# Two-block model forward pass, feed-forward gate and up blocks: the low half of two of eight chunks made by a negated rounding and an accumulating transfer

## The chip, the core and the metric

The kernel runs on one core of one Trainium2 chip. The metric is the device time of one execution in microseconds, the median of three runs. All arithmetic is in 32-bit floating point; the matrix products run on TensorE in its float32r form, which keeps fewer bits of each factor.

## The reference, cut to what matters

The program computes two layers of a hybrid attention model (`first_block`) and then one layer of another (`second_block`) for 256 tokens of width 2048. The change touches only the last part, the feed-forward network of the second block, with D_FF = 5632:

```python
gt, up = jnp.split(rms_norm_2(x, g_ffn) @ w_gate_up, 2, axis=-1)
return x + (jax.nn.silu(gt) * up) @ w_down
```

Everything before it (projections, attentions, gates) is many products of the same kind, activations times a streamed weight matrix.

## The kernel before, in words

**Tiles.** A block is 512 output columns of one weight matrix for all 256 tokens. Its weights are streamed in chunks. A plain chunk of 512 KB holds two row groups of 128 rows by 512 columns, 1024 numbers on each of 128 partitions. The gate and up blocks (names `gt` and `up`, 11 each) have 8 chunks, s = 0 to 7; the down blocks (4 for each j) have 2.

**Two halves.** To be as exact as the reference, each number w is split into a high half, w rounded to float32r, and a low half, w minus the high half. A product is three matmuls: activations' high half by the weights' high half, high by low, and low by high. A chunk is thus 2 row groups x 2 token groups x 3 = 12 matmuls of 128x128 by 128x512.

**One chunk's way.** SP (`load`, L698 on) brings the raw weights into one of four raw slots. ScalarE (`split`, L1108 on, instruction at L1121) writes the high half into `w_hi`. VectorE (`split`, L1408 on, instruction at L1418) subtracts it from the raw weights and writes the low half into `w_lo`. TensorE (L1100) multiplies. All four engines count: `raw_landed` per slot, `hi_done`, `lo_done` and `mm_done` over all chunks. Raw, `w_hi` and `w_lo` each have four slots in this stage, so that chunk c+4 uses the slots of chunk c. ScalarE waits for `mm_done` of chunk c-4 before it writes the halves of chunk c; TensorE waits for `lo_done` of chunk c; SP waits, before it loads into a raw slot, for `lo_done` of the chunk that was in it. SP issues the loads strictly in order, and stands at the first one whose wait is not met.

**Order of the feed-forward blocks.** gate 0, up 0; then for j = 0 to 8 gate j+1, the four down blocks of j, up j+1; then gate 10, up 10, down 9, down 10. In all 22 x 8 + 44 x 2 = 264 chunks. Other work is put between chunks by a schedule written out by hand (`schedule`): after an up block, `h_feed` turns (transposes) its product on TensorE (L808, four matmuls) after the next block's s = 2 and s = 3, and ScalarE and VectorE copy it. Each engine does read-outs of finished blocks after it has split the chunk four further on.

**The start of the stage.** The scale of the norm before the feed-forward network comes from the squares of x. ScalarE takes them in four parts (`x_sq`, L1267) as the last output blocks end, the last part at the second chunk of gate 0. GpSimd then computes the scale in `x_norm(3)`, four small instructions, the last thing that its program does. It is needed only when gate 0 is read out. Turns of x (`x_feed`) come after s = 1 and s = 2 of gate 0. GpSimd issues no transfer anywhere in the kernel.

Of the kernel before, what the change touches and what calls it, by code (L numbers as in the profile page):

```python
# [201 lines left out]
SPLIT_OF = {r: c for c, (_b, _w, _s, r) in enumerate(UNITS) if r is not None}  # L202
R_BEHIND = [max(U_PREV[:c + 1]) for c in range(N_CHUNKS)] + [N_CHUNKS]
BEHIND = {c: range(max(R_BEHIND[c], 0), R_BEHIND[c + 1]) for c in range(N_CHUNKS)}
EXT_FIRST = {l: [min(c for c in range(FIRST_WIDE[l], N_CHUNKS) if U_SLOT[c] == k) for k in (4, 5)] for l in range(DEPTH)}
EXT_LOAD = {l: min(r for r, (b, _s) in enumerate(LOADS) if b >= FIRST_PANEL[l] and R_SLOT[r] >= RING) for l in range(DEPTH)}
BLOCK = {b.name: i for i, b in enumerate(BLOCKS)}
# [3 lines left out]
def end_of(*name):  # L211
    return BLOCKS[BLOCK[name]].end
# [197 lines left out]
def hybrid_program(nc, x, mem_by_col, w_in, w_mem_kv, w_branch, w_out, w_in2, b_gate, w_uq, w_ukv, w_o_mla, w_o_dil, w_o2, w_gu, w_down,  # L410
                   pars_d, x_by_col, k_ident, k_levels, k_tables, k_dil, x_kept, mkv_kept, out):
    with ExitStack() as ctx:
# [162 lines left out]
        sums_done, forms_ready, forms_done, form_rounded = sem("sums_done"), sem("forms_ready"), sem("forms_done"), sem("form_rounded")  # L575
        crossed, x_banks_free, wide_sig = sem("crossed"), sem("x_banks_free"), sem("wide_sig")
        hi_done, lo_done, mm_done = sem("hi_done"), sem("lo_done"), sem("mm_done")
        gm_free = [sem(f"gm_free{i}") for i in range(2)]
        pt_full, pt_hi = sem("pt_full"), sem("pt_hi")
        pt_free = [sem(f"pt_free{i}") for i in range(2)]  # L580
# [114 lines left out]
        def _(sp):  # L695
            def load(r):
                b, s = LOADS[r]
                blk = BLOCKS[b]  # L698
                if R_PREV[r] >= 0:
                    sp.wait_ge(lo_done, SPLIT_OF[R_PREV[r]] + 1)  # L700
                    if LOADS[R_PREV[r]] in LOAD_SUMS:
                        sp.wait_ge(sums_done, 2 * LOAD_SUMS[LOADS[R_PREV[r]]] + 2)
                if r in EXT_LOAD.values():
                    sp.wait_ge(y_ready, Y_OF["s_pv", "m", blk.name[1], H - 1] + 1)
                k = R_SLOT[r]
                to = slot_of(raw, raw_more, k)[:, 0:blk.ck * blk.width].rearrange("p (j n) -> p j n", n=blk.width)
                sp.dma_start(to, cut(weights[blk.weights], blk.ck)[s, :, :, blk.col:blk.col + blk.width]).then_inc(raw_landed[k], 16)
# [15 lines left out]
                sp.dma_start(rows(x_kept)[:, :, n * NB:(n + 1) * NB], xs[:, :, n * NB:(n + 1) * NB]).then_inc(x_saved, 16)  # L723

            def back(l):
                sp.wait_ge(lo_done, SUMS_UNIT[LAST_PANEL[l], SEVEN[-1]] + 1)
                if l:
                    sp.wait_ge(x_saved, 64 * l)
                sp.dma_start(xs, rows(x[0] if l == 0 else x_kept)).then_inc(x_back, 16)
# [6 lines left out]

            def bring_mkv():
                sp.wait_ge(mkv_out, 16)
                sp.wait_ge(lo_done, end_of("merge", 0, "b", 3))
                sp.dma_start(arena[:, 11408:13456].rearrange("p (i n) -> p i n", n=NB),  # L740
                             mkv_kept.rearrange("i (t p) n -> p (i t) n", p=P)).then_inc(mkv_in, 16)

# [57 lines left out]
        def _(pe):  # L800
# [235 lines left out]
            def panel(b, blk):  # L1036
                l, n = blk.name[1], PANEL_N[b]
                if n:
                    pe.wait_ge(x_banks_free, 2 * n)
                if b == FIRST_PANEL[l]:  # L1040
                    turned(pe, PT_OF["tail", "b", l, H - 1])
                    pe.wait_ge(ps_free, PS_OF["b_qk", l, H - 1] + 1)
                    pe.wait_ge(y_ready, Y_OF["norm", "b", l, H - 1] + 1)
                    pe.wait_ge(forms_done, len(SEVEN) * (l + 1))
                for c in range(blk.first, blk.end):
                    _b, what, s, _r = UNITS[c]
                    first, last = s == SEVEN[0], s == SEVEN[-1]
                    pe.wait_ge(lo_done, c + 1)
                    if what == "low":
                        three(PT[0], *by_token(2 * s + 1, 0), c, 0, False, False)  # L1050
                        mm = three(PT[1], *by_form(s, 3), c, 1, False, False)
                    elif what == "first":
                        if first:
                            pe.wait_ge(gm_free[0], blk.before[0])
                        mm = three(G[0][:, 0, :], *by_token(2 * s, 0), c, 0, first, last)
                    elif what == "sums13":
                        three(G[0][:, 1, :], *by_form(s, 0), c, 0, first, last)
                        if first:
                            pe.wait_ge(gm_free[1], blk.before[1])
                        mm = three(G[1][:, 0, :], *by_form(s, 2), c, 1, first, last)  # L1060
                    elif what == "sums24":
                        three(G[1][:, 1, :], *by_form(s, 1), c, 0, first, last)
                        mm = three(PS, *by_token(2 * s + 1, 1), c, 1, False, False)
                    else:
                        end = s == KD - 1
                        for t, banks in enumerate(((PT[0], PT[1]), (PS, PO))):
                            for h, bank in enumerate(banks):
                                mm = three(bank, *by_token(s, t), c, h, c == blk.first, end)
                    mm.then_inc(mm_done, 1)
                    between(c)  # L1070

            for b, blk in enumerate(BLOCKS):
                if blk.kind == "panel":
                    panel(b, blk)
                    continue
                ah, al = (xh, xl) if blk.pair == "x" else (yh, yl)
                if blk.before[blk.g]:
                    pe.wait_ge(gm_free[blk.g], blk.before[blk.g])
                for s in range(blk.chunks):
                    c = blk.first + s  # L1080
                    fed = need(blk.name, s)
                    if fed:
                        turned(pe, PT_OF[fed])
                    if blk.name == ("mk", 0):
                        pe.wait_ge(mem_fed, s + 1)
                    if blk.name == ("a_qi", 0):
                        pe.wait_ge(first_fed, s + 1)
                        pe.wait_ge(ident_in, 16)
                    pe.wait_ge(lo_done, c + 1)
                    for j in range(blk.ck):  # L1090
                        k = s * blk.ck + j
                        if blk.kind == "turned":
                            for q, (a, w) in enumerate(((ah, high_of), (ah, low_of), (al, high_of))):
                                mm = M.matmul(G[blk.g][0:blk.width, 0, 0:T], ringed(w, blk, c)[:, j, :], a[:, blk.kk + k, :],  # L1094
                                              start=(k == 0 and q == 0), stop=(k == blk.kt - 1 and q == 2))
                            continue
                        for t in range(TT):
                            tok = slice(t * P, (t + 1) * P)
                            for q, (a, w) in enumerate(((ah, high_of), (ah, low_of), (al, high_of))):
                                mm = M.matmul(G[blk.g][:, t, :], a[:, blk.kk + k, tok], ringed(w, blk, c)[:, j, :],  # L1100
                                              start=(k == 0 and q == 0), stop=(k == blk.kt - 1 and q == 2))
                    mm.then_inc(mm_done, 1)
                    between(c)

        @block.scalar
        def _(act):
            A = nc.scalar.activation

            def split(c):
                b, what, s, r = UNITS[c]  # L1110
                if r is None:
                    act.wait_ge(sums_done, 2 * SUMS_N[b, s] + (1 if what == "sums13" else 2))
                else:
                    act.wait_ge(raw_landed[R_SLOT[r]], 16 * (R_COUNT[r] + 1))
                if U_PREV[c] >= 0:
                    act.wait_ge(mm_done, U_PREV[c] + 1)
                for l in range(DEPTH):
                    if c in EXT_FIRST[l]:
                        act.wait_ge(y_ready, Y_OF["norm", "b", l, H - 1] + 1)
                        act.wait_ge(o_squared, NORM_OF["norm", "b", l, H - 1] + 1)  # L1120
                A(high_of(c)[:, 0:size_of(c)], source_of(c), ACT.Copy).then_inc(hi_done, 1)  # L1121

            def stem(b):
                _, l, br, m = BLOCKS[b].name
# [259 lines left out]
        def _(dve):  # L1384
# [9 lines left out]
            def sums13(n, r):  # L1394
                for k in (r, r + 1):
                    dve.wait_ge(raw_landed[R_SLOT[k]], 16 * (R_COUNT[k] + 1))
                if n >= 2:
                    dve.wait_ge(lo_done, SUMS_UNIT[SUMS[n - 2]] + 1)
                q = pair_of(r)
                V.tensor_tensor(sums[:, n % 2, 0:2, :], q[:, :, 1, :], q[:, 0, :, :], ALU.subtract).then_inc(sums_done, 1)  # L1400

# [5 lines left out]

            def split(c):  # L1408
                b, what, s, r = UNITS[c]
                if what == "low":  # L1410
                    sums13(SUMS_N[b, s], r - 1)
                elif what == "first":
# [329 lines left out]
        def _(pool):  # L1742
# [149 lines left out]
            for i in range(2):  # L1892
# [2 lines left out]
                    freed(pool, BLOCK[f"ukv{2 * i + j}", 2])  # L1895
                head_norm(f"k{i}", 2, k_h[:, :, 4 * i:4 * i + 4, 0:P], 4)
            x_norm(3)


def packed(inputs):  # L1900
# [33 lines left out]
```

## Time and profile before

| | |
|---|---|
| median of 3 runs | 3288.4 us (3288.28 to 3288.69) |
| span of the profiled execution | 3286.7 us |
| TensorE busy | 3274.1 us, 100% |
| VectorE busy | 2052.8 us, 62% |
| ScalarE busy | 1577.0 us, 48% |
| GpSimd busy | 307.5 us, 9% |
| HBM traffic | 188 GB/s over the span |

The span is from the first to the last instruction in the profile; it lies 1.7 us under the median of the runs. TensorE's matmuls are pipelined, so the busy time of one (0.39 us) overlaps the next; the time from start to start is the pace. "L1100" is line 1100 of the kernel.

### The profile page before, as it was taken

Reading aid. Unit: us, or ns where it says so; the run is one execution under the profiler, and the core shown is the slowest. Engines: PE = TensorE matmul, PEld = TensorE weight load, DVE = VectorE, ACT = ScalarE, POOL = GpSimd, SP = SyncE. Lnnn points to the kernel's source line nnn. Section 1 sums busy time; section 2 is a strip of 40 time slices with the busy share of each in tenths; the row PEclk is TensorE's granted clock in tenths of the full one; section 3 lists DMA queues with packets and bytes.
Section 4 is the critical chain, followed back from the end, with each engine's and each line's share of the span. In section 5 each row is a group of like instructions: output and inputs, shape, how many; then the busy total and the mean of one; then the engine's idle time right before and its main releaser. Section 6 shows DMA issues by size and latency. Waiting matters only on the chain.

```text
span 3286.7 us, 39565 instructions
## 1 busy us (share of the span) xinstructions
PE 3274.1 (100%) x15172; PEld 2714.8 (83%) x15172; DVE 2052.8 (62%) x2284; ACT 1577.0 (48%) x1992; POOL 307.5 (9%) x267
## 2 busy tenths in 40 slices
PE   9999999999999999999999999999999999999999
PEld 7888888888888888888888888888888888888887
DVE  5466655588865656555888655575555555555555
ACT  6454445455544444454555445455444444444443
POOL 0111241100001102411000010160000000000000
PEclk9999999999999999999999999999999999999999
DMA  8665555665656655556666675554665666666665
GB/s 300 193 185 165 166 175 162 192 209 189 228 182 200 184 167 167 172 165 190 201 202 201 202 219 168 167 180 151 194 191 184 187 191 192 192 187 191 192 192 167
DMA packets 303805, 619.76 MB, mean 189 GB/s; under 512 B 24960, under 2 KB 29440, under 8 KB 302464
## 3 DMA queue, kind: packets, MB, share of 16 engines
q1 hardware_dynamic: 303616, 617.22, 61.4%
q8 instruction: 121, 1.98, 0.2%
q14 instruction: 68, 0.56, 0.1%
HBM read 609.80 MB, written 7.34 MB: 188 GB/s over the span
## 4 chain that ended last, share of the span: by engine, by line
PE 100%; DMA 0%; DVE 0%; ACT 0%; SPq 0%; issue 0%
PE G L1100 80%; PE X L1025 3%; PE X L1027 3%; PE X L1026 3%; PE X L808 2%; PE G L1027 1%; PE G L1026 1%; PE G L1025 1%; PE X L921 1%; PE X L893 1%; PE G L1094 1%; PE X L948 0%; PE X L947 0%; PE X L914 0%; PE X L895 0%; PE X L868 0%
## 5 line engine op out<-in xcount | busy, mean ns | idle before, releaser
L1418 DVE TENSOR_TENSOR w_lo<-raw,w_hi 128x1024 fp32r<-128x1024 f32 (+1 forms) x1016 | 1255.4, 1237 | 1149.1 <-ACT w_hi L1121 1125.9
L1121 ACT ACTIVATE w_hi<-raw 128x1024 fp32r<-128x1024 f32 (+1 forms) x1016 | 1067.1, 1052 | 1448.8 <-PE G L1100 1376.5
L1100 PE MATMUL G<-w_hi,xh 128*128 128x512 f32 x2560 | 1021.8, 399 | 0.0
L1100 PE MATMUL G<-w_hi,xl 128*128 128x512 f32 x2560 | 999.4, 390 | 0.0
L1100 PE MATMUL G<-w_lo,xh 128*128 128x512 f32 x2560 | 996.9, 389 | 0.0
L1100 PEld LDWEIGHTS G<-w_hi,xl 128*128 128x128 f32 x2560 | 480.5, 188 | 103.6
L1100 PEld LDWEIGHTS G<-w_hi,xh 128*128 128x128 f32 x2560 | 481.1, 188 | 95.6 <-issue 2.7
L1100 PEld LDWEIGHTS G<-w_lo,xh 128*128 128x128 f32 x2560 | 481.6, 188 | 94.3
L1100 PE MATMUL G<-w_hi,yh 128*128 128x512 f32 x1256 | 497.3, 396 | 8.2 <-DVE w_lo L1418 8.2
L1100 PE MATMUL G<-w_hi,yl 128*128 128x512 f32 x1256 | 490.7, 391 | 0.0
L1100 PE MATMUL G<-w_lo,yh 128*128 128x512 f32 x1256 | 489.7, 390 | 0.0
L1100 PEld LDWEIGHTS G<-w_hi,yh 128*128 128x128 f32 x1256 | 236.5, 188 | 55.0 <-issue 8.2
L1100 PEld LDWEIGHTS G<-w_hi,yl 128*128 128x128 f32 x1256 | 236.2, 188 | 50.5
L1100 PEld LDWEIGHTS G<-w_lo,yh 128*128 128x128 f32 x1256 | 236.6, 188 | 47.5
L1025 PE MATMUL X<-w_hi,xh 128*128 128x512 f32 x340 | 132.8, 390 | 0.0
L1027 PE MATMUL X<-w_hi,xl 128*128 128x512 f32 x340 | 132.7, 390 | 0.0
L1026 PE MATMUL X<-w_lo,xh 128*128 128x512 f32 x340 | 132.4, 389 | 0.0
L1759 POOL TENSOR_TENSOR stat<-stat 128x4 f32<-128x4 f32 x4 | 0.8, 203 | 1250.6 <-ACT core L1267 1250.6
L1418 DVE TENSOR_TENSOR w_lo<-raw_more,w_hi 128x1024 fp32r<-128x1024 f32 (+1 forms) x56 | 64.9, 1165 | 27.6 <-ACT w_hi L1121 27.6
L1121 ACT ACTIVATE w_hi<-raw_more 128x1024 fp32r<-128x1024 f32 (+1 forms) x56 | 56.2, 1014 | 48.6 <-PE X L1027 38.3
L808 PE MATMUL X<-ident,arena 128*128 128x128 f32 x512 | 77.1, 272 | 0.0
L808 PEld LDWEIGHTS X<-ident,arena 128*128 128x128 f32 x512 | 63.3, 140 | 15.2
(248 smaller groups left out, 2782.2 us busy)
## 6 DMA issues: line engine op xcount, KB each, us to landing
raw<-in_w_in SPq DMA_DIRECT2D x572, 512.0 KB, 3.6
raw<-in_w_gate_up SPq DMA_DIRECT2D x176, 512.0 KB, 3.6
raw<-in_w_down SPq DMA_DIRECT2D x88, 512.0 KB, 3.6
raw<-in_w_out SPq DMA_DIRECT2D x64, 512.0 KB, 3.9
raw_more<-in_w_in SPq DMA_DIRECT2D x52, 512.0 KB, 4.3
raw<-in_w_branch SPq DMA_DIRECT2D x48, 512.0 KB, 3.9
raw<-in_w_mem_kv SPq DMA_DIRECT2D x32, 512.0 KB, 6.0
raw<-in_w_o SPq DMA_DIRECT2D x32, 512.0 KB, 3.7
```

The source lines that it names most:

```text
L808: mm = M.transpose(PT[i % 2][0:n, col:col + P], src, ident[:])
L893: mm = M.matmul(PS[:, t * T:(t + 1) * T], qk_t[:, t * P:(t + 1) * P], qk_t[:, T:2 * T], start=True, stop=br != "l")
L921: mm = M.matmul(PO[:, t * P:(t + 1) * P], p_t[:, a, t * P:(t + 1) * P], v(a), start=(a == 0), stop=(a == TT - 1))
L1025: M.matmul(bank, of_h, high_of(c)[:, cols], start=start, stop=False)
L1026: M.matmul(bank, of_h, low_of(c)[:, cols], start=False, stop=False)
L1027: return M.matmul(bank, of_l, high_of(c)[:, cols], start=False, stop=stop)
L1094: mm = M.matmul(G[blk.g][0:blk.width, 0, 0:T], ringed(w, blk, c)[:, j, :], a[:, blk.kk + k, :], start=(k == 0 and q == 0), stop=(k == blk. ...
L1100: mm = M.matmul(G[blk.g][:, t, :], a[:, blk.kk + k, tok], ringed(w, blk, c)[:, j, :], start=(k == 0 and q == 0), stop=(k == blk.kt - 1 and ...
L1121: A(high_of(c)[:, 0:size_of(c)], source_of(c), ACT.Copy).then_inc(hi_done, 1)
L1418: V.tensor_tensor(low_of(c)[:, 0:n], source_of(c), high_of(c)[:, 0:n].bitcast(F32), ALU.subtract).then_inc(lo_done, 1)
L1759: link(V.tensor_tensor(s[:, 0:4], s[:, 0:4], s[:, 4:8], ALU.add))
```

## The change

In each gate and up block, chunks s = 2 and s = 6 (`ADDED`, 44 in all) get their low half another way. VectorE skips them. ScalarE, right after the high half, writes the rounded weights once more with scale -1 into `w_lo` and counts `lo_negative`. GpSimd, after everything else in its program, waits for that count and issues a transfer from the raw slot to `w_lo` that adds what it brings to what is there, so that w_lo becomes raw minus high half. Its landing adds 16 to `lo_added`. TensorE waits for `lo_added` at these chunks, and SP waits for it before it loads into their raw slots. As VectorE now counts 44 chunks fewer, every other wait on `lo_done` goes by `lows(n)`, n less the added chunks before n.

```diff
+ADDED = [c for c, (b, _w, s, _r) in enumerate(UNITS) if BLOCKS[b].name[0] in ("gt", "up") and s % 4 == 2]
+ADDED_N = {c: i for i, c in enumerate(ADDED)}
+def lows(n):
+    return n - sum(1 for c in ADDED if c < n)
...
                 if R_PREV[r] >= 0:
-                    sp.wait_ge(lo_done, SPLIT_OF[R_PREV[r]] + 1)
+                    if SPLIT_OF[R_PREV[r]] in ADDED_N:
+                        sp.wait_ge(lo_added, 16 * (ADDED_N[SPLIT_OF[R_PREV[r]]] + 1))
+                    else:
+                        sp.wait_ge(lo_done, lows(SPLIT_OF[R_PREV[r]] + 1))
...
-                    pe.wait_ge(lo_done, c + 1)
+                    if c in ADDED_N:
+                        pe.wait_ge(lo_added, 16 * (ADDED_N[c] + 1))
+                    else:
+                        pe.wait_ge(lo_done, lows(c + 1))
...
                 A(high_of(c)[:, 0:size_of(c)], source_of(c), ACT.Copy).then_inc(hi_done, 1)
+                if c in ADDED_N:
+                    A(low_of(c)[:, 0:size_of(c)], source_of(c), ACT.Copy, scale=-1.0).then_inc(lo_negative, 1)
...
             def split(c):
                 b, what, s, r = UNITS[c]
+                if c in ADDED_N:
+                    return
...
             x_norm(3)
+            for i, c in enumerate(ADDED):
+                pool.wait_ge(lo_negative, i + 1)
+                V.dma_start(low_of(c).bitcast(F32), source_of(c), accum_op=ALU.add).then_inc(lo_added, 16)
```

## Rows read from the trace of the kernel before

**Rows 1.** The page, part 1: busy us, share of the span, instructions.
```profile
PE 3274.1 (100%) x15172; PEld 2714.8 (83%) x15172; DVE 2052.8 (62%) x2284; ACT 1577.0 (48%) x1992; POOL 307.5 (9%) x267
```

**Rows 2.** The page, part 4: the chain that ended last, by engine.
```profile
PE 100%; DMA 0%; DVE 0%; ACT 0%; SPq 0%; issue 0%
```

**Rows 3.** Waits, whole span: who waited for whom, us, times, longest.
```profile
PE G L1100 <- DVE w_lo L1418: 8.2, 1, 8.2
```

**Rows 4.** Waits between 2562 and 3260 us, all that is listed.
```profile
ACT w_hi L1121 <- PE G L1100: 405.3, 253, 2.0
DVE w_lo L1418 <- ACT w_hi L1121: 300.5, 253, 1.8
```

**Rows 5.** The chain in order of time: start, us, what, matmuls.
```profile
2675.22 62.59 PE G L1100 x276
```

**Rows 6.** Timeline: start, us, engine, line, one subtraction and matmuls around it.
```profile
2587.49 1.23 DVE L1418 TENSOR_TENSOR w_lo<-raw,w_hi 128x1024 fp32r<-128x1024 f32 x1 [1.50 <-ACT w_hi L1121]
2587.50 0.39 PE L1100 MATMUL G<-w_hi,xh 128*128 128x512 f32 x1
...
2587.73 0.39 PE L1100 MATMUL G<-w_lo,xh 128*128 128x512 f32 x1
...
2588.86 0.39 PE L1100 MATMUL G<-w_hi,xh 128*128 128x512 f32 x1
...
2589.09 0.39 PE L1100 MATMUL G<-w_lo,xh 128*128 128x512 f32 x1
```

**Rows 7.** Timeline of ScalarE; in brackets its idle time and releaser.
```profile
2602.72 1.06 ACT L1121 ACTIVATE w_hi<-raw 128x1024 fp32r<-128x1024 f32 x1 [1.66 <-PE G L1100]
2605.44 1.06 ACT L1121 ACTIVATE w_hi<-raw 128x1024 fp32r<-128x1024 f32 x1 [1.66 <-PE G L1100]
2606.41 0.58 ACT L1216 ACTIVATE yh<-X 128x512 fp32r<-128x512 f32 x1
```

**Rows 8.** Transfers, whole span: queue, count, KB each, median us to landing.
```profile
arena<-x_kept SPq DMA_DIRECT2D x2, 2048.0 KB, 9.2
...
out<-arena SPq DMA_DIRECT2D x4, 512.0 KB, 2.7
...
tables<-const_dil SPq DMA_DIRECT2D x1, 512.0 KB, 7.3
```

**Rows 9.** The weight loads (line 707) between 2675 and 2741 us.
```profile
L707 SPq DMA_DIRECT2D raw<-in_w_gate_up x16: 367/367/368, 2691.3 to 2732.1; - x16
...
DMA to landing us min/median/max: 3.5/3.7/4.1
```

**Rows 10.** Timeline of GpSimd: first and last instruction of x_norm(3).
```profile
2560.66 0.20 POOL L1759 TENSOR_TENSOR stat<-stat 128x4 f32<-128x4 f32 x1 [345.36 <-ACT core L1267]
...
2561.55 0.70 POOL L1754 TENSOR_TENSOR stat<-stat 128x2 f32<-128x2 f32 x1
```

**Rows 11.** One period of 24 chunks: busy us, clock, DMA share, GB/s.
```profile
2675.00:2741.24 66.24, 66.24 (x300) 54.86 (x297) 37.81 (x34) 27.59 (x29) 0.00 (x0) 1.00 0.64 191
```

**Rows 12.** Timeline of ScalarE at the start of gate 0.
```profile
2558.24 1.06 ACT L1121 ACTIVATE w_hi<-raw 128x1024 fp32r<-128x1024 f32 x1 [1.67 <-PE G L1100]
...
2560.34 0.19 ACT L1267 ACTIVATION_READ_ACCUMULATOR core<-arena 128x1 f32 x1
```

**Rows 13.** The chain around gate 0's s = 2.
```profile
2551.78 6.36 PE G L1100 x28
2558.14 0.44 PE X L808 x4
2558.58 2.76 PE G L1100 x12
```

**Rows 14.** Timeline of TensorE's matmuls at the kernel's start.
```profile
8.19 0.77 PE L1100 MATMUL G<-w_hi,yh 128*128 128x512 f32 x1 [8.19 <-DVE w_lo L1418]
8.75 0.63 PE L1100 MATMUL G<-w_lo,yh 128*128 128x512 f32 x1
9.18 0.63 PE L1100 MATMUL G<-w_hi,yl 128*128 128x512 f32 x1
...
12.16 0.41 PE L1100 MATMUL G<-w_hi,yh 128*128 128x512 f32 x1
12.42 0.39 PE L1100 MATMUL G<-w_lo,yh 128*128 128x512 f32 x1
```

More of the change, by code:

```diff
@@ L577, in hybrid_program @@
         hi_done, lo_done, mm_done = sem("hi_done"), sem("lo_done"), sem("mm_done")
+        lo_negative, lo_added = sem("lo_negative"), sem("lo_added")
         gm_free = [sem(f"gm_free{i}") for i in range(2)]
@@ L725, in back @@
             def back(l):
-                sp.wait_ge(lo_done, SUMS_UNIT[LAST_PANEL[l], SEVEN[-1]] + 1)
+                sp.wait_ge(lo_done, lows(SUMS_UNIT[LAST_PANEL[l], SEVEN[-1]] + 1))
                 if l:
@@ L738, in bring_mkv @@
                 sp.wait_ge(mkv_out, 16)
-                sp.wait_ge(lo_done, end_of("merge", 0, "b", 3))
+                sp.wait_ge(lo_done, lows(end_of("merge", 0, "b", 3)))
                 sp.dma_start(arena[:, 11408:13456].rearrange("p (i n) -> p i n", n=NB),
@@ L1088, in _ @@
                         pe.wait_ge(ident_in, 16)
-                    pe.wait_ge(lo_done, c + 1)
+                    if c in ADDED_N:
+                        pe.wait_ge(lo_added, 16 * (ADDED_N[c] + 1))
+                    else:
+                        pe.wait_ge(lo_done, lows(c + 1))
                     for j in range(blk.ck):
@@ L1397, in sums13 @@
                 if n >= 2:
-                    dve.wait_ge(lo_done, SUMS_UNIT[SUMS[n - 2]] + 1)
+                    dve.wait_ge(lo_done, lows(SUMS_UNIT[SUMS[n - 2]] + 1))
                 q = pair_of(r)
```

## The prediction

> **What bounds the kernel now.** I read the busy shares, the chain that ended last, the waits, and then the timelines of the feed-forward stage, engine by engine. TensorE is busy for 3274.1 of 3286.7 us and the chain runs through it alone [rows 1, 2]. Its one wait for VectorE's low half is the 8.2 us before the first chunk of the whole kernel [rows 3]. From 2562 to 3260 us, nearly all of the changed stage, no wait of TensorE is listed: what is listed there is ScalarE waiting for TensorE to free a w_hi slot, 253 times [rows 4]. So VectorE's subtraction is not late anywhere that this change touches it. The stage runs at TensorE's own pace: 276 matmuls in 62.59 us, 0.2268 us each [rows 5], so a chunk (12 matmuls) takes 2.72 us and four take 10.88. The pitch is the same beside a VectorE subtraction (2587.50 to 2587.73) and after it (2588.86 to 2589.09) [rows 6].
>
> **How much lead a low half has.** With four slots, chunk c's rounding starts 0.1 us after chunk c-4's last matmul, three chunks (8.16 us) before TensorE wants chunk c. Today high half 1.06 plus low half 1.23 us leave well over 5 us of cover.
>
> **What the change removes.** 44 VectorE subtractions (22 blocks x 2) of 1.23 us, 54 us of an engine that waits for ScalarE anyway. On the path they are worth 0, hidden behind TensorE's 100%. I bound the gain by the pitch below (second rival).
>
> **What it adds on ScalarE.** 44 negated roundings of 1.06 us. Back to back, ScalarE's next instruction starts 0.97 us after the first [rows 7], so the negated half is ready 0.97 + 1.06 + 0.07 for the semaphore = 2.1 us after the rounding starts. ScalarE idles 1.66 us between roundings, so 1.06 more fits. Behind it are queued the read-outs and transposed copies of h; those are wanted chunks later, cost 0.
>
> **What it adds on GpSimd and the DMA.** 44 accumulating transfers of 512 KB. Call D the time from GpSimd being free to issue until the sum has landed. The trace has no accumulating transfer and no transfer issued by GpSimd, so D is bounded by rows. Below: the fastest 512 KB landing, the output's 2.7 us [rows 8]. Above: the 2 MB copy, 9.2 us for four times the bytes; another 512 KB table took 7.3 [rows 8]. For the value: the weight loads of this stage land in 3.7 us [rows 9]. Between 512 KB and 2 MB that is (9.2 - 3.7) / 3 = 1.83 us per 512 KB over a fixed 1.9. An addition must read both operands, twice the bytes: 1.9 + 2 x 1.83 = 5.5. GpSimd's small instructions take 0.2 us [rows 10]; I add that for issuing and take D = 5.7 as an estimate. The engines are there: DMA share is 0.64 in this stage [rows 11], and while an accumulation runs SP stands behind it (below), so it runs nearly alone.
>
> The doubling agrees with the Trainium skill, Collectives: The Full Stack, Stop 4, which says a reduction costs "two source reads" and puts the slowdown there, not in the adder. Against it stands DMA: Bandwidth & Descriptors, the SWDGE anatomy, with about 2.0 us plus bytes over 436 GB/s, and no charge for adding: 3.2 us. No row here can show either; by that formula everything below the first chunk would be hidden, which is the first rival.
>
> **The first added chunk is certain to stall.** GpSimd's program issues the transfers after x_norm(3), which needs ScalarE's last squares, which end at 2560.5 [rows 12], and itself ends at 2561.55 + 0.70 = 2562.25 [rows 10]. The first added chunk is s = 2 of the first gate block, and TensorE starts it at 2558.58 (its s = 1 ends at 2558.14, a turn of 0.44 follows) [rows 13]. Nothing upstream of x_norm(3) needs that chunk, so it isn't a deadlock, but TensorE stands still from 2558.58 to 2562.25 + D: 3.67 + 5.7 = 9.4 us. After the 8.19 us of standing still at the kernel's start the matmuls came 0.43 us apart, 512 columns at the 1.2 GHz level, until 12.16 and 0.23 apart after it [rows 14]; the nine from 8.19 to 12.16 took 3.97 us instead of 2.04. I charge the same 1.9 here. Sum: 11.3 us. Nothing later gives it back, since TensorE has no idle time to give.
>
> **The other 43.** Two tests, in the lead's terms. The slot path: 0.1 + 2.1 + D against 8.16, so an undisturbed chunk is late by D - 5.9. The raw path: the next load into this raw slot (chunk c+4) now waits in SP for lo_added, and c+4 is again an added chunk (s = 2, 6, 2, 6), also from one block into the next. From one sum landed to the next: 0.1 + 3.7 load + 0.1 + 2.1 + D = D + 6.0 against 10.88, so each further link adds D - 4.9 to the lateness (before, that load went out 2.4 us after the slot came free and landed at 6.2, 4.7 us ahead of its use). SP's loads for the three plain chunks queue behind that wait, but their halves have 5 us of cover, cost 0. In a gate block after an up block two turns (0.88 us) lie between s = 2 and s = 6, so that link adds D - 5.8. A down block's eight plain chunks end the run. The order of blocks gives gate 0, up 0, gate 1 (six links), eight times up, gate (four), then up 9, gate 10, up 10 (six).
> At D = 5.7 a run of four: -0.2, then 0.6, 1.4, 1.3: TensorE loses 1.4, eight times, 11.2. The first run, after its stall: its second link has one turn, 0.4, then 1.2, 2.0, 2.8, 2.7: 2.8. The last: -0.2, 0.6, 1.4, 1.3, 2.1, 2.9: 2.9. Together 16.9 us.
>
> **Sum.** 11.3 + 16.9 = 28.2 us on a span of 3286.7; the profiled span lies 1.7 us under the runs' median of 3288.4, and I carry that over: 3316.6. The sum is steep in D. At 4.9 and under only the first stall is left; at 7.3 the terms are 12.9 + 8 x 7.7 + 10.7 + 12.5 = 98, so 3386; at 9.2 they are 14.8 + 8 x 15.3 + 20.2 + 23.9 = 181, so 3470.
>
> **Rivals.**
> First, the transfer is covered: D at most 4.9. Then the loss is 3.67 + D + 1.9, at D = 4 some 9.6: 3298 (3297 to 3299). For it: the output's 2.7 us. Against: it has to read twice and no load here lands under 3.5 [rows 9].
> Second, on the other side, not slower: TensorE's pitch of 0.227 us is over the 0.213 that 0.427 at the lower clock level [rows 14] halves to. If VectorE's port traffic made that difference, quiet chunks would gain 12 x 0.0135 = 0.16 us each, 7 us over 44 chunks, 43 over all 264 of the stage. It decides once more than 70 chunks speed up, since the first stall costs 11.3; with all 264 it gives 3288.4 + 11.3 - 43 = 3257 where the transfers are covered. Against: the pitch does not move when VectorE stops within a chunk [rows 6], and VectorE is relieved in 44 chunks only.
> Third, the adding is slow: D above 6.5, so nearly all links are late, 3350 to 3470; 3386 at the 7.3 row. For it: an adder's rate and the software side of GpSimd's queue show in no row. TensorE idling a few us over and over could bring the lower clock level back each time, which adds to it.
>
> **Chances.** The forecast (D 4.9 to 6.5, 3299 to 3350) 0.45; covered, 0.25; slow adding, 0.26; not slower, 0.04. The measurement tells 0.2%, 6.6 us, from no change: faster 0.01, same 0.03, slower 0.96. The range: from 3296 (D near 3 and a milder clock) to 3410 (D near 7.7), leaving about 0.04 below and 0.15 above.
>
> **What would show it.** A TensorE gap before gate 0's s = 2 that ends D after x_norm(3), and matmuls 0.43 us apart behind it. Waits of TensorE for the transfer, longest at the end of a run of added chunks, none in down blocks. ScalarE's rounding of the later links waiting for the raw load, not for TensorE. 44 fewer VectorE subtractions with an unchanged pitch of 0.227. Wrong would be: no gap there (the first term), a GpSimd transfer that lands outside 4.9 to 6.5 us (the second), or a pitch that moved.

## The result, and the profile after

The changed kernel takes 3302.8 us (median of four, 3300.1 to 3303.4) against 3288.55: 14.3 us more, a ratio of 1.0041 (95% interval 1.0030 to 1.0053). The direction and the stall at the first added chunk came as forecast, the losses at the other 43 mostly did not; the whole is half of the 28.2 us that the sum gave. The profiled execution has a span of 3300.6 us.

The page of the changed kernel, against [rows 1, 2]: part 1 (busy us, share, instructions), GpSimd's queue from part 3 (packets, MB, share of the 16 engines), the chain by engine from part 4, and from part 6 the transfers (KB each, median us to landing).

```profile
PE 3278.6 (99%) x15172; PEld 2718.6 (82%) x15172; DVE 1999.7 (61%) x2240; ACT 1617.5 (49%) x2036; POOL 345.7 (10%) x311
...
q0 software_dynamic: 6336, 23.07, 3.7%
...
PE 97%; DMA 2%; ACT 1%; issue 0%; DVE 0%; POOL 0%; SPq 0%; ACTq 0%; POOLq 0%
...
raw<-in_w_gate_up SPq DMA_DIRECT2D x176, 512.0 KB, 4.4
...
w_lo<-raw POOLq DMA_DIRECT2D x44, 512.0 KB, 4.5
```

VectorE has 44 instructions and 53 us less, ScalarE 44 more, and a second queue carries 23 MB. What is new for the time is the 2% of the chain that hangs on a transfer. It lies in few places. The waits between 2562 and 3275 us, where [rows 4] had none of TensorE's (PEld is TensorE's weight load, which meets the wait first; the two rows are the same stalls):

```profile
ACT w_hi L1137 <- PE G L1116: 312.8, 215, 11.6
ACT w_hi L1137 <- DMA raw<-in_w_gate_up: 51.7, 22, 3.3
...
PEld G L1116 <- DMA w_lo<-raw: 11.4, 6, 8.6
PE G L1116 <- DMA w_lo<-raw: 8.9, 2, 8.4
```

**The first added chunk.** The chain in order of time (start, us, what) runs where the prediction drew it: ScalarE's last squares, GpSimd's four instructions of x_norm(3), the transfer, and only then s = 2 of gate 0:

```profile
2559.81 1.33 ACT core L1285 x4
...
2562.15 0.65 POOL stat L1774
2562.80 4.72 DMA w_lo<-raw
2567.52 0.04 issue
2567.56 5.49 PE G L1116 x12
2573.05 0.55 PE X L821 x4
```

Before, TensorE started this chunk 0.44 us after s = 1 and spent 2.76 us on it [rows 13]. Here s = 1 ends at 2558.58 and the turn, 0.44 us as before, at 2559.02, so it stands still 8.5 us, and the 12 matmuls then take 5.49. The windows of TensorE's granted clock say why (us, busy of PE, PEld, DVE, ACT, POOL, then clock, DMA share, GB/s):

```profile
2567.56:2573.36 5.80, 5.80 (x17) 4.54 (x17) 0.00 (x0) 0.00 (x0) 0.00 (x0) 0.52 0.84 283
2573.60:2617.19 43.59, 43.59 (x195) 36.03 (x194) 18.24 (x18) 22.46 (x24) 3.45 (x4) 1.00 0.74 216
```

0.52 is the 1.2 GHz level. Chunk and turn take 5.80 us where they took 3.20, so the clock costs 2.6 and the place 8.5 + 2.6 = 11.1 us.

**The other 43.** From 2620.8 to 2661.7, and again over most of the stage, TensorE runs without a stall. One period of 24 chunks, against [rows 11]:

```profile
2875.00:2941.24 66.24, 66.24 (x297) 54.88 (x296) 32.99 (x30) 31.37 (x33) 3.78 (x5) 1.00 0.76 225
```

VectorE is busy 5 us less, the DMA share is up from 0.64 to 0.76, TensorE is full as before. And 276 matmuls of one stretch take 62.60 us (62.59 in [rows 5]): the pitch has not moved. Five short waits of the weight load follow the first one; four of them show between matmuls, 0.2 to 0.7 us each, 1.5 in all, with some 0.1 us of a slower first matmul behind each. Matched one by one with the matmuls of the kernel before, those of this execution lose 2.0 us between the first added chunk and the end. The prediction expected the longest waits at the end of a run of added chunks; of these four only the one at 2692.6 is there. The chain into it:

```profile
2664.19 5.07 DMA w_lo<-raw
2669.25 0.02 issue
2669.27 3.89 DMA raw<-in_w_gate_up
2673.16 0.02 issue
2673.19 1.06 ACT w_hi L1137
2674.25 0.96 ACT w_lo L1139
2675.20 0.28 issue
2675.49 4.51 DMA w_lo<-raw
2680.00 0.02 issue
2680.02 4.00 DMA raw<-in_w_gate_up
...
2686.43 6.16 DMA w_lo<-raw
2692.59 0.04 issue
```

This is the raw path, link by link: sum landed, load 3.9 to 4.0, two roundings 2.0, release of GpSimd 0.3 to 0.4, sum 4.5. From 2669.25 to 2680.00 is 10.75 us against the 10.88 that TensorE takes for four chunks. A link of ordinary length thus adds nothing. The long sums make the stall: had the last one taken 4.5 us and not 6.16, or the first 4.5 and not 5.07, the 0.3 us for which TensorE stands still at 2692.6 would be covered.

### The profile page after: what moved, and what is told of

It reads as the page before. It is cut to its first block, busy times and chain, and to the rows that moved or that the text cites. A ratio compares the mean times of both kernels' runs of the same rounds, so it can differ in the third digit from the quotient of the medians.

```text
span 3300.6 us, 39565 instructions
## 1 busy us (share of the span) xinstructions
PE 3278.6 (99%) x15172; PEld 2718.6 (82%) x15172; DVE 1999.7 (61%) x2240; ACT 1617.5 (49%) x2036; POOL 345.7 (10%) x311
## 4 chain that ended last, share of the span: by engine, by line
PE 97%; DMA 2%; ACT 1%; issue 0%; DVE 0%; POOL 0%; SPq 0%; ACTq 0%; POOLq 0%
PE G L1116 78%; PE X L1038 3%; PE X L1040 3%; PE X L1039 3%; PE X L821 2%; DMA w_lo<-raw 1%; PE G L1040 1%; PE G L1039 1%; PE G L1038 1%; DMA raw<-in_w_gate_up 1%; PE X L934 1%; PE X L906 1%; PE G L1110 1%; PE X L961 0%; PE X L960 0%; PE X L927 0%
## 5 line engine op out<-in xcount | busy, mean ns | idle before, releaser
L1438 DVE TENSOR_TENSOR w_lo<-raw,w_hi 128x1024 fp32r<-128x1024 f32 (+1 forms) x972 | 1201.3, 1238 | 1165.5 <-ACT w_hi L1137 1142.2
L1920 POOL DMA_DIRECT2D w_lo<-raw x44 | 38.4, 872 | 640.2 <-ACT w_lo L1139 640.2
```

What stands on the lines that cost most here:

```text
L1438: V.tensor_tensor(low_of(c)[:, 0:n], source_of(c), high_of(c)[:, 0:n].bitcast(F32), ALU.subtract).then_inc(lo_done, 1)
L1920: V.dma_start(low_of(c).bitcast(F32), source_of(c), accum_op=ALU.add).then_inc(lo_added, 16)
```

## The experiments

Each is the changed kernel with the edit shown. Times are medians. The kernel before was timed beside each: 3288.55 for the first four, 3288.65 for "The same, unchained" and for the chunk at s = 4, and 3288.87 for the other four.

**GpSimd's order.**
```diff
-            x_norm(3)
             for i, c in enumerate(ADDED):
+                if i == 1:
+                    x_norm(3)
                 pool.wait_ge(lo_negative, i + 1)
```


> All 44 added chunks stay; GpSimd issues the first transfer before x_norm(3) instead of after it. Theory A (of the 14.3 us lost, 11.2 are the first chunk: 8.5 us standing behind x_norm(3) and 2.6 us at the lower clock level; the rest is the links of the raw slot): that gap is gone and the total is 3291.5 (3290 to 3293). Rival B (the loss is spread over the 44 transfers: issue, contention, pitch): the gap's place changes little, 3300 or more.

Measured: 3292.0 us, ratio 1.0009 (1.0000 to 1.0019). The transfer goes out at 2552.44, x_norm(3) follows, the long gap is gone. Moving one line of GpSimd's program gives back 10.8 of the 14.3 us.

**The first chunk alone.**
```diff
-... s % 4 == 2]
+... s % 4 == 2][:1]
```


> Only the first of the 44 chunks (s = 2 of gate 0) is made by the transfer, the other 43 by VectorE as before. A: 3288.5 + 11.2 = 3299.7, TensorE idle 8.5 us once and 12 matmuls 0.43 us apart. B (loss spread over 44): 3289.

Measured: 3299.5 us, 1.0033 (1.0020 to 1.0046): 11.0 us from one transfer. That this equals the 11.1 us of the changed kernel is in part chance. In this profile TensorE stands still for the same 8.5 us, but only six matmuls run slowly, from 2567.85 to 2570.58, and not the whole chunk and the turn:

```profile
2570.15 0.63 PE L1116 MATMUL G<-w_hi,xl 128*128 128x512 f32 x1
2570.58 0.46 PE L1116 MATMUL G<-w_hi,xh 128*128 128x512 f32 x1
2570.87 0.39 PE L1116 MATMUL G<-w_lo,xh 128*128 128x512 f32 x1
```

So the lower clock costs 1.3 us here and 2.6 there. Another 0.9 us of this execution's loss was there before the changed stage began (see the last part of the account below).

**All but the first.**
```diff
-... s % 4 == 2]
+... s % 4 == 2][1:]
```


> The first of the 44 chunks goes back to VectorE, the other 43 keep the transfer. A: only the later links are left, 3288.5 + 1.9 to 3.0 = 3291, no fall of the clock. B: 3302.

Measured: 3290.5 us, 1.0006 (0.9997 to 1.0015). Forty-three transfers cost 1.9 us (1.4 by the matmuls of the profile), and 11.0 + 1.9 is 12.9 of 14.3. The spread loss (B) falls three times over.

**No two in a row.**
```diff
-... s % 4 == 2]
+... s == 2][1:]
```


> Added chunks only at s = 2 of each gate and up block, and not in gate 0: 21 transfers, never two in a row on one raw slot. A, with chaining through the raw slot as the cause of the later stalls: none is left, 3288.5 (within 0.5). Rival C (the later stalls come from the slot path alone, each transfer now and then landing late): half of them stay, 3289.5 to 3290.

Measured: 3290.0 us, 1.0003 (0.9994 to 1.0013), where I had expected 3288.5 from chaining and 3289.5 to 3290 from single late landings. By the time this one leans to rival C, but 1 us is at the edge of what these runs tell: in the profiled execution (3290.8 us) 1.4 us of the difference lie ahead of the changed stage and 0.8 in it. The profile is the firmer evidence. It has one stall on a transfer, and no chain can lead to it, so A's "none is left" does not hold:

```profile
PEld G L1116 <- DMA w_lo<-raw: 0.9, 1, 0.9
```

**The lead cut by one rounding.** This puts the other 43 back to about the D that the prediction assumed.
```diff
                 if c in ADDED_N:
+                    A(low_of(c)..., source_of(c), ACT.Copy, scale=-1.0).then_inc(neg_once, 1)
+                    act.wait_ge(neg_once, ADDED_N[c] + 1)
                     A(low_of(c)..., source_of(c), ACT.Copy, scale=-1.0).then_inc(lo_negative, 1)
```


> ScalarE writes the negated rounding of each added chunk twice, one after the other with a semaphore between, so each transfer starts some 1.15 us later; nothing else changes. This sets the lead back to about what the prediction assumed (its D of 5.7 against some 4.85 now, release included). A (chained links: load 3.9 to 5.1 + 2.1 + 0.35 + 4.5 + 1.15 against 10.88, each link adding 1.2 to 2.3 us): runs of four lose 3 to 4 us each and the runs of six 5 to 7, in all 3302.8 + 30 to 40, 3333 to 3343; by the prediction's own terms at D = 6.0, 3329. Rival C (only the slot path matters, 7.0 + 1.15 against 8.16): at most 0.1 per chunk, 3304 to 3307.

Measured: 3331.8 us, 1.0130 (1.0115 to 1.0145), 29.0 us over the changed kernel. A's 30 to 40 was a little high; C is far off. The prediction's own terms with D = 6.0 (4.5 + 0.35 + 1.1 as measured) give 0.1, 1.2, 2.3, 2.5 for a run of four, 4.2 and 4.7 for the long runs, 28.9 together; with the first stall of 11.1, which is not delayed by this, 3328.6. The later links measured 43.0 - 11.1 = 31.9 us over the kernel before, so the terms come out 3 us short. The waits of this kernel between 2560 and 3322 us:

```profile
ACT w_hi L1137 <- PE G L1116: 241.4, 166, 11.3
ACT w_hi L1137 <- DMA raw<-in_w_gate_up: 105.0, 32, 4.5
...
PEld G L1116 <- DMA w_lo<-raw: 44.2, 39, 8.6
```

39 waits instead of 6, and ScalarE waits twice as long for raw loads: those are the chained links.

**The same, unchained.** Both roundings, but only s = 2 and not in gate 0.

> The doubled negated rounding with 21 added chunks only (s = 2 of each block but gate 0), so that no two added chunks follow each other on one raw slot. A (the 29 us that the doubling cost with 44 chunks came through the chain sum, raw load, roundings, sum): an unchained chunk is at its limit, 8.2 against 8.16, loses 0 to 0.3: 3290.0 + 0 to 5, 3290 to 3295. Rival C (each delayed transfer costs by itself, 29 us over 43): 14 us, 3304.

Measured: 3295.2 us, 1.0019 (1.0009 to 1.0028), at the edge of what A allowed, and 8.8 us under C. Its waits between 2560 and 3280 us:

```profile
PEld G L1116 <- DMA w_lo<-raw: 7.9, 21, 0.6
```

All 21 are now late, by 0.38 us on average, the slot path at its limit. The prediction's terms give 0.1 us for such a chunk. The second rounding costs (3295.2 - 3290.0) / 21 = 0.25 us per chunk here and 29.0 / 43 = 0.67 in the chained kernel: the greater part of the loss there comes through the chain.

**What D is made of.** A copy in place of the addition:
```diff
-... source_of(c), accum_op=ALU.add).then_inc(lo_added, 16)
+... source_of(c)).then_inc(lo_added, 16)
```


> The 44 transfers copy the raw weights over w_lo instead of adding them: same bytes written, the addition and its second read left out (the low half is then wrong in value, the timing path the same). A (adding costs a second read, a 4 KB packet of 340 ns being two of 170): packets near 170 ns, issue to landing 3.1 instead of 4.5 us, the first gap 1.4 shorter, later stalls gone: 3299 to 3300. Rival D (340 ns is what a transfer from slot to slot issued by GpSimd costs): 4.5 us and 3302 to 3303 as before.

Measured: 3296.9 us, 1.0027 (1.0016 to 1.0038), below the forecast of 3299 to 3300. In the profile (3298.5 us) TensorE waits for a transfer once, at the first chunk, for 7.0 us; the later stalls are gone, as forecast. Nine matmuls run slowly there, fewer than in the changed kernel. Why the executions lie as far apart as 3296.4 and 3299.2 us no trace shows. Its line 1920, then the same for the changed kernel (duration ns min/median/max):

```profile
L1920 POOL DMA_DIRECT2D w_lo<-raw x44: 530/530/782, 2563.2 to 3236.6; - x44
...
DMA to landing us min/median/max: 2.8/2.9/5.2
```
```profile
L1920 POOL DMA_DIRECT2D w_lo<-raw x44: 852/862/1094, 2562.8 to 3240.5; - x44
...
DMA to landing us min/median/max: 4.5/4.5/6.2
```

A 4 KB packet takes a median of 160 ns copied and 340 ns added. A transfer has 128 of them, eight for each of the 16 engines if they are spread evenly: by that estimate the addition costs 8 x 0.18 = 1.4 us there, beside 0.33 us in issuing; between the landings lie 1.6 us.

**Half the bytes.**
```diff
-... low_of(c).bitcast(F32), source_of(c), accum_op ...
+... low_of(c)[:, 0:NB].bitcast(F32), source_of(c)[:, 0:NB], accum_op ...
```


> The 44 transfers add only the first 512 of the 1024 columns (the rest of the low half keeps the negated high half: its value is wrong). Splits the 4.5 us: A (1.43 to the first packet, 8 packets one after the other, 0.3 to the count, a packet's time going by its bytes): 2 KB packets of 170 ns, landing at 3.1 us. Rival D (time per packet fixed): 340 ns and 4.5 us.

Measured: landing at 3.3 us, 2 KB packets of 187 ns, issuing unchanged at 862 ns, 3298.5 us. Time goes mostly by bytes (A), with a small part per packet: 340 is less than 2 x 187. Here too TensorE waits for a transfer only once, at the first chunk.

**Where the clock falls.** One added chunk only, at s = 3, then at s = 4.
```diff
-... s % 4 == 2]
+... s == 3][:1]
```


> One added chunk only, s = 3 of gate 0 (not s = 2). TensorE reaches it at about 2562.2, the sum lands at 2567.5: idle 5.3 us. If the lower clock level follows that too: 3288.5 + 5.3 + 2.6 = 3296.4; if it does not: 3293.8.

> One added chunk only, s = 4 of gate 0. TensorE reaches it at about 2564.9, the sum lands at 2567.3: idle 2.4 us. After 8.5 and 5.3 us idle the matmuls came 0.427 us apart; if that follows an idle time this short too, 3288.6 + 2.4 + 2.6 = 3293.6, if not 3291.0 to 3291.5.

Measured: 3297.6 us (1.0026, 1.0015 to 1.0037) and 3291.7 us (1.0009, 1.0000 to 1.0019). The first matmul after the gap and the clock behind it, s = 3 and then s = 4:

```profile
2566.84 0.80 PE L1116 MATMUL G<-w_hi,xh 128*128 128x512 f32 x1 [5.22 <-DMA w_lo<-raw]
...
2566.84:2572.13 5.29, 5.29 (x12) 4.13 (x13) 0.00 (x0) 0.00 (x0) 0.00 (x0) 0.50 0.77 266
```
```profile
2567.58 0.50 PE L1116 MATMUL G<-w_hi,xh 128*128 128x512 f32 x1 [2.44 <-DMA w_lo<-raw]
...
2567.58:2572.00 4.42, 4.42 (x19) 3.67 (x20) 0.00 (x0) 0.87 (x1) 0.00 (x0) 1.00 0.76 254
```

After 5.2 us of standing still the next matmuls ran at 1.2 GHz; after 2.4 us they did not, here.

No version beat the kernel before. The best one that keeps transfers, at s = 2 alone, comes within 1.4 us of it. VectorE is not on the chain [rows 2], so relieving it makes nothing there shorter.

## Why the prediction was half right

**What bounds the kernel: right.** 44 subtractions fewer on VectorE bought nothing; the pitch stayed at 62.60 us for 276 matmuls. The rival of a faster pitch is refuted.

**The first chunk: right.** Forecast 11.3 us (9.4 idle, 1.9 clock), measured 11.1 in the profile (8.5 and 2.6) and 11.0 by the kernel that has this chunk alone. Two errors nearly cancel: D was too long, and I took the nine slow matmuls of the kernel's start where the whole chunk and the turn ran slow. That the sum comes this near is luck, for the second term is not fixed: with this chunk alone it was 1.3 us.

**The other 43: the step that failed is the size of D.** The prediction put 5.7 us; measured are 4.5 us from GpSimd's start to landing, and 0.3 to 0.4 us before it from ScalarE's end, together about 4.85. I had charged 0.07 of that wait separately. The term was 16.9 us and measured 1.9 (all but the first) to 3.5 (all, with the order changed), 1.4 to 2.0 by the matmuls of the profiles. The prediction had itself named a landing outside 4.9 to 6.5 us as a sign that this term is wrong. My formula for links has its threshold at D = 4.9, and 4.85 is just under it: with the right D it says that nothing is late, which is the rival that I gave 0.25. So the path was drawn rightly, and the value of D stood on the wrong side of a threshold. The kernel with the second rounding shows that the arithmetic nearly holds: at D = 6.0 it gives 28.9 us for the later links, and 31.9 were measured. The time still lies in the forecast's band of 3299 to 3350 us, though D does not, and that is luck too: the rival's sum at the measured D is 10.3 us, and the longer slow stretch and the few late landings, which that rival did not have, carried it over 3299.

**Why D was too long.** Doubling for the addition was right in size: 340 against 160 ns a packet. No run tells a second read from the adder itself. What I doubled was wrong. I drew the 1.83 us per 512 KB out of the 2 MB copy's 9.2 us [rows 8], a transfer that shared its engines with the weight loads. The packets say less: eight of 340 ns are 2.7 us where I charged 2 x 1.83 = 3.7. The fixed part was about right: 4.5 - 2.7 = 1.8 plus 0.35 of release, against the 1.9 + 0.2 I took. For a plain copy the output's 2.7 us was the nearer row: a copy between two slots landed in 2.9.

The Trainium skill, Collectives: The Full Stack, says that a reduction is slower because the add needs two source reads; it says so in the section on the bandwidth ceiling, not in Stop 4 as the prediction has it. The traces fit that (340 against 160 ns). By the formula of the Trainium skill, DMA: Bandwidth & Descriptors, in its anatomy of a DMA on the SWDGE path, I estimate 3.2 us; the plain copy's 2.9 lies near it, the addition's 4.5 does not. The verdict drawn from it, all covered behind the first chunk, was nevertheless nearly the measured one.

**What is left of the later stalls.** They need a late landing. In the changed kernel all four that show between matmuls have one in their chain: two sums of 6.2 us (at 2686.4 and 3139.9) and two raw loads of 5.1 and 4.9 us (at 3000.4 and 3056.4). During all four an instruction packet of 16 KB was on one of the engines. The transfers between 2686.4 and 2692.7 us, which spans one late sum, and for comparison between 2675.45 and 2680.05, a punctual one:

```profile
q0 software_dynamic: 144, 0.52, 44.0%
q1 hardware_dynamic: 140, 0.25, 10.6%
q8 instruction: 1, 0.02, 1.7%
```
```profile
q0 software_dynamic: 144, 0.52, 60.1%
q1 hardware_dynamic: 166, 0.31, 18.1%
```

Such a packet took 0.9 to 1.8 us and came about every 28 us; TensorE waits for all 16 counts of a sum, so one late share is enough to hold it up. Four cases are few, but the traces of the six kernels with many adding transfers hold 217 sums, whose last packet usually ended 4.2 us after the issue. For the 16 with such an instruction packet in their time it ended at 4.5 to 6.0 us; of the other 201, 13 were more than 0.25 us late and none ended after 4.8. This is read from traces: no run took the instruction packets away, so that they cause the late landings is likely and not shown.

**Where the rest of the 14.3 us lies.** The first chunk alone and all the others alone leave 1.4 us of it. Set side by side matmul by matmul, the changed kernel's profiled execution is already 0.6 us behind the kernel before at 2556 us, where no changed chunk has run yet; then come 11.2 us at the first chunk and 2.0 us after it, which makes the 13.9 us between the two spans. In the other profiles this early difference lies between 0.3 us ahead and 1.4 us behind, and it arises in the first 50 us of the kernel, long before any transfer is issued; so differences of 1 us between these medians should not be read closely.

## What to carry to other kernels

Before work is moved to an idle engine's queue, read what already stands in that queue at that time: one transfer behind an unrelated norm cost about four fifths of what this change lost, and a moved line gave it back. Where a new operation has no row, set its chance by where the thresholds of the lead lie, not by a middle value; and take its rate from single packets of an undisturbed transfer rather than from the landing of a big one that shares its engines. A buffer that is freed later than before couples each use to the next through its reload, so test spacing as well as count.

## What was not expected of the hardware

An adding packet cost 2.1 times a copying one (340 and 160 ns for 4 KB), and GpSimd took 862 ns to issue the adding transfer and 530 ns the copying one. The first transfer of a kernel took 0.23 us longer to issue (1.09 us). TensorE fell to 1.2 GHz after 5.2 us of standing still and not after 2.4, and after 8.5 us of it TensorE stayed there for six matmuls in one execution and for twelve and the turn in another. And instruction packets of 16 KB share the DMA engines with the data, up to 1.8 us on one of them.
